# A rotary swap on VectorE in place of TensorE, and three projection chunks moved into the first attention steps

## What is computed

```python
h = rms_norm(x, norm_mix_pre)
proj = h @ w_in                      # 1536 columns: qa 512, ka 128, va 128, qb 512, kb 128, vb 128
qa, ka = apply_rope(rms_norm(qa, q_norm_a), ang_axial), apply_rope(rms_norm(ka, k_norm_a), ang_axial)
qb, kb = apply_rope(qb, ang_1d), apply_rope(kb, ang_1d)
out_a = softmax(qa ka^T / 8) va      # 8 heads of 64, all 512 keys, 2 key heads
out_b = softmax(qb kb^T / 8) vb      # 8 heads of 64, keys within 128 positions, a sink per head

def apply_rope(x, ang):              # halves of the 64 features of a head
    x1, x2 = jnp.split(x, 2, axis=-1)
    return jnp.concatenate([x1 * cos - x2 * sin, x2 * cos + x1 * sin], axis=-1)
```

## Time and profile before

| | |
|---|---|
| span of the profiled execution | 1365.9 us |
| own time of the profiled execution outside the span | not given; the three runs lie 1.2 to 5.6 us above the span |
| instructions | 14667 |
| TensorE matmul busy | 1331.7 us, 97% |
| VectorE busy | 677.9 us, 50% |
| ScalarE busy | 534.2 us, 39% |
| mean granted TensorE clock | 0.994 of full |
| share of TensorE in the chain that ended last | 93% |

### The profile page before, as it was taken

How to read it: one execution, slowest core, us unless ns; L and a number is a source line. 1 busy time by engine, 2 the same in 40 slices (tenths; PEclk the granted TensorE clock), 3 DMA queues, 4 the chain that set the end, 5 groups by cost and what they waited for, 6 DMA issues and landing times.

```text
span 1365.9 us, 14667 instructions
## 1 busy us (share of the span) xinstructions
PE 1331.7 (97%) x6082; PEld 1054.7 (77%) x6082; DVE 677.9 (50%) x922; ACT 534.2 (39%) x717; POOL 114.3 (8%) x112
## 2 busy tenths in 40 slices
PE   7998989999999999999999999999999999999996
PEld 5763448888888888887888888788888888888875
DVE  6868774665444442126534445664554444423346
ACT  6537774543223232225225555543332232322232
POOL 3000012510000000103000001012000000001012
PEclk9999999999999999999999999999999999999998
DMA  6110003123322222322321111222222222223221
GB/s 244 62 62 1 1 1 123 63 93 104 111 94 93 93 78 92 106 95 69 131 93 63 62 62 62 93 93 93 95 102 112 93 93 93 80 90 106 95 93 62
DMA packets 21586, 117.74 MB, mean 86 GB/s; under 512 B 2448, under 2 KB 4880, under 8 KB 10896
## 3 DMA queue, kind: packets, MB, share of 16 engines
q1 hardware_dynamic: 20400, 114.53, 23.8%
q10 hardware_dynamic: 1120, 2.27, 0.5%
HBM read 114.70 MB, written 2.10 MB: 86 GB/s over the span
## 4 chain that ended last, share of the span: by engine, by line
PE 93%; DVE 4%; ACT 1%; DMA 1%; issue 0%; SPq 0%; DVEq 0%; ACTq 0%
PE ps L465 92%; PE ps L671 2%; DMA w_raw<-weights 1%; DVE nmax L1495 1%; DVE prob L1307 1%; DVE w_lo L1303 0%; DVE OUT L1310 0%; DVE h_lo L1310 0%; DVE hf L1303 0%; DVE X L1303 0%; ACT hf L890 0%; ACT sq L890 0%; ACT w_hi L890 0%; DVE diag L1307 0%; ACT h_hi L890 0%
## 5 line engine op out<-in xcount | busy, mean ns | idle before, releaser
L465 PE MATMUL ps<-h_hi,w_hi 128*128 128x512 f32 (+1 forms) x1256 | 496.5, 395 | 11.8 <-DVE w_lo L1303 10.7
L465 PE MATMUL ps<-h_lo,w_hi 128*128 128x512 f32 (+1 forms) x1256 | 488.8, 389 | 0.0
L465 PE MATMUL ps<-h_hi,w_lo 128*128 128x512 f32 (+1 forms) x1256 | 488.5, 389 | 0.0
L1303 DVE TENSOR_TENSOR w_lo<-w_raw,w_hi 128x2048 fp32r<-128x2048 f32 (+2 forms) x117 | 242.0, 2071 | 268.8 <-ACT w_hi L890 268.7
L465 PEld LDWEIGHTS ps<-h_hi,w_hi 128*128 128x128 f32 x1256 | 236.5, 188 | 67.4 <-issue 15.2
L890 ACT ACTIVATE w_hi<-w_raw 128x2048 fp32r<-128x2048 f32 (+2 forms) x117 | 201.2, 1721 | 193.4 <-DMA w_raw<-weights 193.3
L465 PEld LDWEIGHTS ps<-h_lo,w_hi 128*128 128x128 f32 x1256 | 236.7, 188 | 51.1 <-issue 3.4
L465 PEld LDWEIGHTS ps<-h_hi,w_lo 128*128 128x128 f32 x1256 | 236.7, 188 | 49.2
L440 POOL TENSOR_TENSOR sqsum<-sqsum,sq 128x512 f32<-128x512 f32 x66 | 95.9, 1453 | 953.6 <-ACT sq L890 951.8
L465 PE MATMUL ps<-mid_lo,w_hi 128*128 128x512 f32 x352 | 136.9, 389 | 0.0
L465 PE MATMUL ps<-mid_hi,w_hi 128*128 128x512 f32 x352 | 136.9, 389 | 0.0
(11 more groups left out here) (180 smaller groups left out, 1093.3 us busy)
## 6 DMA issues: line engine op xcount, KB each, us to landing
w_raw<-weights SPq DMA_DIRECT2D x81, 1024.0 KB, 4.8
w_raw<-weights SPq DMA_DIRECT2D x32, 704.0 KB, 3.9
X<-x_t SPq DMA_DIRECT2D x3, 512.0 KB, 7.7
c<-constants ACTq DMA_DIRECT2D x1, 1280.0 KB, 8.4
w_raw<-weights SPq DMA_DIRECT2D x4, 256.0 KB, 8.2
wp_raw<-weights SPq DMA_DIRECT2D x1, 1024.0 KB, 6.9
out_t<-OUT SPq DMA_DIRECT2D x2, 512.0 KB, 2.9
X<-x_t SPq DMA_DIRECT2D x2, 256.0 KB, 3.9
```

The costliest lines, as they stand in the source:

```text
L465: return nc.tensor.matmul(out, lhsT, rhs, start=start, stop=stop, skip_group_check=loose)
L1303: return nc.vector.tensor_tensor(out, a, b, op)
```

## The change

Three things change.

1. **The swap.** The 64 features of a head are put in another order on the partitions (`HEAD_ROWS`, applied to the weights' columns, the tables and the gains on the host), so that the partner of each feature lies 16 lanes off within the same 32 lanes. The swap is then one VectorE `stream_shuffle` of 128x512 for each roped chunk; the sign sits in the sine table. All ten rotation matmuls go.
2. **The late chunks.** Projection chunks 9, 10 and 11 no longer run ahead of the attention steps. `scores(0)` follows chunk 8; chunk 9 is issued at step 0, the halves of chunk 10 at steps 2 and 4, those of chunk 11 at steps 6 and 8, each ahead of that step's `scores`. `scores(1)` is now ahead of the transposes of step 0. The accumulators of these chunks are banks 7, 6, 7.
3. **Moves.** The rope of chunk 8 is now behind `negmax(1)`. The splits of units 6 and 7 move on VectorE from before the steps to steps 3 and 7, on ScalarE to steps 1 and 7. The ropes of chunks 9 and 10 have four parts each instead of three, at steps 32, 34, 36, 38 and 40, 42, 44, 46 (before: 4, 7, 10 and 15, 18, 21). The transposes of the last value chunk stay at step 23.

```diff
+LATE_BANKS = (7, 6, 7)
+LATE_PARTS = {0: (9, 0, 8), 2: (10, 0, 4), 4: (10, 4, 8), 6: (11, 0, 4), 8: (11, 4, 8)}
+LATE_ROPE, LATE_TR, LATE_V = {9: 32, 10: 40}, 23, 25
+HEAD_ROWS = [HD * (r // HD) + HD // 4 * (r % HD // 32) + (r % 16 if r % 32 < 16 else HD // 2 + r % 16) for r in range(P)]
+PARTNER = [(r + 16) % 32 for r in range(32)]
 # TensorE, item(j)
-                mm(ps[:, rot_bank(j), :], c1[:, C_ROT - C1_AT:C_ROT - C1_AT + P], y_of(j)).then_inc(rot_done, 1)
 # TensorE, projection and steps
-            for u in range(1, UNITS_IN1):
-                unit("in1", u, 2 * u, 2, KS, h_hi, h_lo, after=beside, hooks={3: {3: eps_row}, 11: {4: lambda: scores(0)}})
+            for u in range(1, UNITS_IN1 - 1):
+                unit("in1", u, 2 * u, 2 if u < 4 else 1, KS, h_hi, h_lo, after=beside, hooks={3: {3: eps_row}})
+            scores(0)
+            def late_part(j, k0, k1):
+                u = j // 2
+                if k0 == 0:
+                    if j == 9:
+                        pe.wait_ge(*n_mix_pre.factor_used)
+                    elif j == 10:
+                        pe.wait_ge(lo_ready, u)
+                        pe.wait_ge(hvar_ready, len(NORMED))
+                    else:
+                        pe.wait_ge(evac_act, EVAC["in1", 9][1])
+                for k in range(k0, k1):
+                    last = three(BANK["in1", j], u % SLOTS, j % 2 * KD + k, h_hi[:, k, :], h_lo[:, k, :],
+                                 k == 0, k == KD - 1)
+                if k1 == KD:
+                    last.then_inc(group_done, 1)
             for s, (kind, h, b, k0, k1) in enumerate(STEPS):
-                if s and s % 2 == 0:
+                if s in LATE_PARTS:
+                    late_part(*LATE_PARTS[s])
+                if s % 2 == 0:
                     scores(s // 2 + 1)
 ...
-                if s == 0:
-                    scores(1)
 # VectorE, rope(j)
-                stt(straight, y_of(j), scale, c1[:, cos:cos + S], ALU.mult, ALU.mult)
-                dve.wait_ge(rot_done, i_roped + 1)
-                m = mark(stt(crossed, ps[:, rot_bank(j), :], scale_rot, c1[:, sin:sin + S], ALU.mult, ALU.mult))
-                dve.wait_ge(dve_self, m)
+                dve.wait_ge(evac_act, EVAC["in1", j][1])
+                m = mark(swapped(crossed, y_of(j)))
+                stt(straight, y_of(j), scale, c1[:, cos:cos + S], ALU.mult, ALU.mult)
+                dve.wait_ge(dve_self, m)
+                link(stt(crossed, crossed, scale_rot, c1[:, sin:sin + S], ALU.mult, ALU.mult))
 # VectorE, order
-            for j in range(1, LATE1):
+            for j in range(1, LATE1 - 1):
                 rope(j)
 ...
             negmax(0)
             negmax(1)
-            split(UNITS_IN1 + 1)
+            rope(LATE1 - 1)
 ...
                 negmax(s + 2)
+                if s in (3, 7):
+                    split(UNITS_IN1 + s // 4)
                 for j, at in LATE_ROPE.items():
-                    for part in range(3):
-                        if s == at + 3 * part:
+                    for part in range(4):
+                        if s == at + 2 * part:
                             late_rope(j, part)
```

More of the change, by code:

```diff
@@ L326, in build @@
                     bank = PLEG_BANKS[j]
+                if phase == "in1" and j >= LATE1:
+                    bank = LATE_BANKS[j - LATE1]
                 BANK[phase, j] = bank
@@ L545, in _ @@
             KS = range(KD)
[L547 to L552, removed]
             def item(j):
-                if j < 0:
-                    return
                 c = ORDER1[j]
[L558 to L564, removed]
                 if c in V1:
+                    pe.wait_ge(evac_act, EVAC["in1", j][1])
                     for b in range(NB):
-                        last = nc.tensor.transpose(ps[:, rot_bank(j), b * P:(b + 1) * P],
+                        last = nc.tensor.transpose(ps[:, vee_bank(j), b * P:(b + 1) * P],
                                                    y_of(j)[:, b * P:(b + 1) * P], ident[:, :])
@@ L596, in scores @@
                     pe.wait_ge(keys_ready, 1)
+                if kind and b == 0:
+                    pe.wait_ge(roped, max(roped_upto(ORDER1.index(6 + c)), roped_upto(ORDER1.index(10))))
                 if t == 16:
-                    pe.wait_ge(roped, len(ROPED))
                     pe.wait_ge(keys_ready, 2)
@@ L659, in _ @@
                     weighted((s - 10) // 8, (s - 10) % 8 // 2)
[L660 to L662 removed]
+                if s == LATE_TR:
+                    item(11)
                 pe.wait_ge(pn_ready, s + 1)
[L664 to L667 removed]
                 if s >= 2:
@@ L1002, in evacuate @@
                 af(y_of(j), ps[:, BANK["in1", j], :], ACT.Copy).then_inc(evac_act, 1)
-            for j in range(11):
-                if j in (3, 5, 7, 9):
+            for j in range(LATE1):
+                if j in (3, 5, 7):
                     split(j // 2 + 2)
                 evacuate(j)
-                if j == 10:
-                    split(UNITS_IN1 + 1)
                 if j == 1:
@@ L1052, in _ @@
                 if s == 1:
+                    split(UNITS_IN1)
+                    evacuate(9)
+                if s == 5:
+                    evacuate(10)
+                if s == 7:
+                    split(UNITS_IN1 + 1)
+                if s == 9:
                     evacuate(11)
@@ L1746, in constants @@
     half = HD // 2
[L1747 to L1751, removed]
     c[:, C_TRI:C_TRI + P] = np.where(i[:, None] >= i[None, :], -1.0, 0.0)
@@ L1766, in constants @@
         ang = np.concatenate([ang.astype(np.float32)] * 4).astype(np.float64)
-        c[:, cos:cos + S], c[:, sin:sin + S] = np.cos(ang), np.sin(ang)
+        sign = np.where(i % HD < half, -1.0, 1.0)[:, None]
+        c[:, cos:cos + S], c[:, sin:sin + S] = np.cos(ang)[HEAD_ROWS], (sign * np.sin(ang))[HEAD_ROWS]
     for g, w in enumerate(POOL_WINDOWS):
@@ L1800 @@
     a = {n: np.asarray(v) for n, v in inputs.items()}
-    w_in = pack(tiles(a["w_in"][0], ORDER1), 16)
+    columns = [P * c + r for c in range(12) for r in (range(P) if c in V1 else HEAD_ROWS)]
+    w_in = pack(tiles(a["w_in"][0][:, columns], ORDER1), 16)
     first = w_in[0]
@@ L1821 @@
     cols += [np.roll(c, HD // 2, axis=0) for c in cols[-2:]]
+    cols[-4:] = [c[HEAD_ROWS] for c in cols[-4:]]
     cols.append(np.broadcast_to(a["sink_b"].reshape(1, NH), (P, NH)))
```

41 lines of the change are left out of this document (21 added, 20 removed).

## The result

The changed kernel takes 1374.26 us (median of 4 runs, 1372.53 to 1376.53) against 1368.85 (4 runs, 1367.03 to 1371.51). The ratio is **1.0041, with a 95% interval of 1.0026 to 1.0057**. That is slower by 0.41%, 5.6 us. The forecast was +1.2 us on the earlier median of 1370.56, so 1371.8. The profiled execution took 1372.53 us; its span is 1370.6 against 1365.9.

A forecast was written before the change was run, and what follows sets the result against it. TensorE, busy 97% of the span, was taken to bound the kernel. The terms, -2.9 + 2.0 - 2.2 + 4.3 = +1.2 us on the median of 1370.56, gave 1371.8 us; the range was 1364 to 1379.

The forecast's parts named there:

- term 6: Steps 32 to 46: eight rope parts at even steps each stop TensorE 0.4 to 0.6 us; +4.3 us, between 2 and 5.
- Term 1: Ahead of chunk 8's end: six rotations fewer on TensorE, 5.16 us, so chunk 8 ends at 70.6.
- Term 2: VectorE's queue ahead of step 0: at 0.65 us a shuffle, TensorE idles 7.2 us before the transposes of step 0.
- rivals of the slow shuffle: VectorE's queue ahead of step 0 and two late steps: shuffle of 1.3 us, 1378.3 us, up to 1389; chance 0.16.
- the work hidden as drawn: Rival, ahead of step 0: ropes keep up, transposes start 7.1 us earlier, no clock fall; 1362.7 us; chance 0.04.
- The shuffle reaches across as meant: Rival claimed the opposite: the swap needs more than one operation; sized as the slow shuffle, no chance of its own.
- Term 3: First ten steps: half chunks add to the loop, pairs take 5.84 us, scores(6) starts at 111.4 against 114.29; -2.9 us.
- Term 4: After the idle time ahead of step 0: the clock falls for a low stretch of 3.5 us; +2.0 us, between 0 and 4.
- The rival of a clock that stays low through these steps: Much of the first ten steps at half clock: +4.8 to +7.2 in place of 2.0, 1374.6 to 1377.0 us; chance 0.1.
- Term 5: Steps 10 to 31: rope parts at steps 10 and 18 and a rotation at 13 go; -2.2 us.
- The first rival: VectorE's slack takes the late parts and the clock stays: Terms 4 and 6 at 0 and 1, 1366.5 us; chance 0.2.
- The rival in which VectorE's slack takes the late parts: The same as the first rival: 1366.5 us, or 1364 with a shuffle at 0.41; chance 0.2.

The follow-up runs named there:

- Experiment 3: Changed kernel with only the variance of chunk 7's rope ahead of the first maxima; its rest, chunk 8's rope and the splits at odd steps: 1366.72 us, 0.9993.
- experiment 4: Changed kernel with scores ahead of the half chunk at steps 0 to 8 instead of behind it: 1369.75 us, ratio 1.0016.
- experiment 5: Changed kernel with GpSimd's three additions cut to 8 of 512 columns, so the norm's sums are incomplete: 1370.05 us, ratio 1.0013.
- experiment 1: The swap alone: the kernel before, in its order of work, with the shuffle and the late ropes in four parts: 1360.81 us, ratio 0.9954.
- experiment 6: Changed kernel with the eight late rope parts at odd steps 11 to 25 in place of even steps 32 to 46: 1364.31 us, ratio 0.9971.
- experiment 7: Changed kernel with late rope parts at odd steps 33 to 47 and GpSimd's additions cut to 8 of 512 columns: 1364.11 us, ratio 0.9973.
- experiment 9: Changed kernel with late rope parts at odd steps 33 to 47, timed again on another chip, twelve executions: 1369.05 us, ratio 1.0013.
- experiment 10: Changed kernel with the edits of experiments 3, 4 and 6, and late ropes of chunks 8, 9 and 10 from steps 11, 19 and 27: 1353.13 us, 0.9892.
- experiment 11: The swap alone as in experiment 1, with late rope parts at odd steps 5 to 11 and 15 to 21: 1358.7 us, ratio 0.9933.
- The second look at the changed kernel: The changed kernel with nothing altered, one more execution: 1373.44 us.
- experiment 2: Changed kernel with the eight late rope parts one step later, at odd steps 33 to 47: 1374.78 us, ratio 1.0043.

## Why the prediction was right and where it wasn't

The forecast said +1.2 us and "No change and 0.3% (4.1 us) can't be told apart here". It came as +5.6 (3.6 to 7.8), which is over 0.3%; the forecast had given that a chance of 0.26, half of what it gave to "same". The range held the time. The terms that were worked out stand, term 6 too once it is measured alone. What made the difference were two effects that had no term: the meeting with GpSimd (+1.8) and the clock late in the attention (+2.6).

- **Term 1, the rotations: right.** Chunk 8 ends at 69.63 against 75.75; less the offset of 0.88 that is -5.24, forecast -5.16.
- **Term 2, VectorE's queue: right.** The shuffle holds VectorE for 0.63 (taken 0.65), and a mask load takes 0.01. TensorE's idle time ahead of step 0 is 6.82 (forecast 7.2). The rivals of the slow shuffle and of the work hidden as drawn fall with it. The shuffle reaches across as meant.
- **Terms 3 and 4, the first ten steps and the clock: right in kind.** The half chunk was added to the loop: pairs of 5.87, forecast 5.84. The clock fell after the idle time. Together -1.3, forecast -0.9. The low clock there lasted 6.8 us (0.8 ahead of 84 and the stretch to 90), twice the 3.5 taken, but part of it fell on idle time. Experiment 3 puts the place at 7.5 us and experiment 4 the loop at 4.5. By the Trainium skill, "TensorE: Matmul & The Clock Gate", "Why this matters for your kernels", idle gaps bring half rate back; the window from 84, at 0.50, agrees. The rival of a clock that stays low through these steps fell: it is back at 1.00 from 90 on.
- **Term 5, steps 10 to 31: right**, -2.19 against -2.2.
- **Term 6, steps 32 to 46: right for the parts alone, too small in this kernel.** "Each part stops it for 0.4 to 0.6 us. The seven other steps read alike": six of them did, for +3.5 us, and with the additions of GpSimd out of the way all eight cost +4.55 (experiment 5), forecast +4.3. But the steps 43 to 46 don't read alike. The three additions of GpSimd lie there, in the trace of before too. The forecast laid the late parts past them without asking what a fuller VectorE queue would meet. In the changed kernel the stops came out at +6.3 (3.5 + 2.8), above the upper bound of 5; the 1.8 over experiment 5 is the meeting. The first rival took 1 as this term's low end where the term's own paragraph says 2; nothing came to hang on it.
- **A term that wasn't there: the clock late in the attention**, 0.7 + 1.9 = +2.6 us up to the output projection. Term 4 priced a fall behind the one idle time that the forecast knew of, although had shown one late in the attention. Cut into stretches of 1 us, the 10.1 us are two pieces: 3.4 us from 175.3 on, behind the long stop, and 6.7 from 182.1 on, just behind sixteen `ones` matmuls of one column each (180.32 to 182). The stop can account for the first piece only. The kernels of experiments 1, 5, 6 and 7, which don't have it, lack the first piece and have the second, from 171.0, 181.2, 175.7 and 176.7 on, between 0.1 us ahead of the end of those matmuls and 1.8 behind it. Before the change, and in the traces of experiments 9, 10 and 11, no fall follows them. What decides on the second piece stays open.
- **Luck.** That the range held the time is luck: its upper end stood for a slow shuffle, which did not come, and not for what did. And -0.9 of the traced difference is the low clock of the first 30 us in the trace of before. It makes the change look better in this pair of traces. The second look at the changed kernel has low time there too, (0.17 + 0.12) x 12 = 3.5 us.
- The rival in which VectorE's slack takes the late parts fell on the order, as argued: the same parts are free at odd steps (experiments 6 and 7; in the latter `scores(16)` to `scores(25)` takes 26.15 us, against 26.43 before).

The rule that the forecast lacked stands in the Trainium skill, "SBUF — State Buffer", "Who interferes with whom". A VectorE operation in a two-port mode or with two inputs in SBUF and a GpSimd operation that reads SBUF lock each other out, the one issued later waits until the other is done, and a reduction never contends. The rows after the change agree: one-source scales (1.47, 1.35) and a two-source rope part (1.60) were held, while the reduction at 170.38 in the kernel before, inside the addition of 169.96 to 171.23, kept its 0.43.
```profile
169.96 1.27 POOL L440 TENSOR_TENSOR sqsum<-sqsum,sq 128x512 f32<-128x512 f32 x1 [91.81 <-ACT sq L890]
```
```profile
170.38 0.43 DVE L1495 TENSOR_REDUCE nmax<-ps 128x1 f32<-128x257 f32 x1 [0.59 <-PE ps L465]
...
170.97 0.47 DVE L1307 TENSOR_SCALAR prob<-prob,rden 128x384 f32<-128x384 f32 x1
...
172.09 0.75 DVE L1307 TENSOR_SCALAR prob<-prob,rden 128x256 f32<-128x256 f32 x1
```
Before the change VectorE issued its scale 1.0 us after the addition had begun and lost 0.05; 0.75 for a scale that takes 0.35 elsewhere was the warning to be read. In the changed kernel a scale is issued 0.02 us behind an addition, and the wait is whole. That the late parts are what shifted it there was not tested by itself; experiment 5 shows the additions' share.

**Open.** What decides, from one execution to the next, whether the clock falls after stops of 0.58 and 0.90 us was not settled; the same program on one chip had both long and short executions. Nor was it shown why the kernels of experiments 1 and 6, without such stops, had 6.7 and 10.3 us of low clock behind the `ones` matmuls, and the kernel before had none there.

## What to carry to other kernels

An operation moved into a loop is priced by its place in the loop's order, not by the average slack of its engine: the same eight parts cost nothing at odd steps and stop TensorE at even ones, and the same half chunks are worth 4.5 us more when they are issued behind the scores. Before work is laid past a stretch on VectorE, look at what GpSimd reads from SBUF there. Ask of the granted clock in the stretches that a change touches, and time a kernel whose clock differs between executions over many of them: five executions put the odd steps at 1.0043, twelve others at 1.0013. A low clock behind a stop in one trace doesn't show that the stop brought it; look at a kernel without the stop.

## What the runs showed of the hardware

- A VectorE shuffle of 128x512 fp32 across lanes within groups of 32 takes 0.72 to 0.75 us busy, 0.62 to 0.64 to the next start; its mask load 0.01.
- A VectorE operation of 0.42 us issued 0.02 us behind a GpSimd addition of 1.27 took 1.47, one of 0.68 issued 0.22 behind 1.60. With an addition of 8 columns they took 0.42 and 0.68. It goes the other way too: in experiment 2 an addition issued 0.20 us behind a two-source operation of VectorE took 1.60 us in place of 1.27.
- From 168 us on, the low clock differed by 17 us (20.5 against 3.4) between two executions of one kernel, and the output projection started 7.7 us later relative to step 0 (211.07 - 85.81 against 204.44 - 86.85).
- Low stretches of 6.7 and 10.3 us came in kernels in which TensorE had waited for no scale for over 30 us (experiments 1 and 6). They began at 171.0 and 175.7, at the end of sixteen `ones` matmuls of one column each and 1.2 us behind it.
